# Down projections of three MLP groups as Strassen-Winograd products in a two-layer fp32 decoder step

## The reference

```python
x = x + mix
h = rms_norm(x, g_mlp[layer])
x = x + jnp.square(jax.nn.relu(h @ w_up[layer])) @ w_down[layer]
```

## Time and profile before

| | us |
|---|---|
| median of 3 runs | 1569.56 (1568.65 to 1571.38) |
| profiled execution, its own time | 1571.89 |
| profiled execution, span | 1570.2 |
| TensorE busy | 1517.2 (97%) |
| VectorE busy | 726.8 (46%) |
| ScalarE busy | 491.9 (31%) |
| GpSimd busy | 117.8 (8%) |
| granted TensorE clock, mean | 0.989 |

### The profile page before, as it was taken

How to read it: one execution, slowest core, us unless ns; L and a number is a source line. 1 busy time by engine, 2 the same in 40 slices (tenths; PEclk the granted TensorE clock), 3 DMA queues, 4 the chain that set the end, 5 groups by cost and what they waited for, 6 DMA issues and landing times.

```text
span 1570.2 us, 33444 instructions
## 1 busy us (share of the span) xinstructions
PE 1517.2 (97%) x13119; PEld 1423.2 (91%) x13119; DVE 726.8 (46%) x1265; ACT 491.9 (31%) x787; POOL 117.8 (8%) x238
## 2 busy tenths in 40 slices
PE   6999999989999999999999999898999999999996
PEld 5999867679999999999999996666999999999996
DVE  4355475635443343333543466764544434334333
ACT  5111254423332131221321116442333313213133
POOL 5310112310000000000010000222000000000000
PEclk9999999999999999999999999999999999999998
DMA  4322577732223222232242237775223222322222
GB/s 132 98 80 79 151 245 251 257 101 82 79 80 94 80 80 82 79 94 81 80 136 80 82 101 238 241 236 163 75 81 87 81 83 78 94 80 81 83 79 74
DMA packets 230949, 178.84 MB, mean 114 GB/s; under 512 B 9320, under 2 KB 202924, under 8 KB 230850
## 3 DMA queue, kind: packets, MB, share of 16 engines
q1 hardware_dynamic: 217154, 137.50, 29.9%
q0 software_dynamic: 13696, 40.00, 8.0%
HBM read 170.20 MB, written 7.26 MB: 113 GB/s over the span
## 4 chain that ended last, share of the span: by engine, by line
PE 91%; DVE 3%; SPq 2%; issue 1%; DMA 1%; ACT 1%; POOLq 0%; POOL 0%; ACTq 0%; DVEq 0%
PE B L1301 70%; PE B L1518 4%; PE B L1530 3%; PE B L1327 2%; PE B L1612 2%; PE B L1574 1%; PE B L1318 1%; PE B L1550 1%; PE B L1561 1%; SPq L382 1%; DMA WR<-in_w_in_even_dram 1%; DVE SK L1194 1%; PE B L1596 1%; PE B L1528 1%; PE B L1400 1%
## 5 line engine op out<-in xcount | busy, mean ns | idle before, releaser
L554 ACT ACTIVATE WH<-WR 128x1024 fp32r<-128x1024 f32 x175 | 184.3, 1053 | 435.1 <-PE B L1301 422.3
L822 DVE TENSOR_TENSOR WL<-WR,WH 128x1024 fp32r<-128x1024 f32 x188 | 230.2, 1224 | 57.8 <-ACT WH L544 29.0
L1301 PE MATMUL B<-ffH,WH 128*128 128x288 f32 x1024 | 219.7, 295 | 0.0
L1301 PE MATMUL B<-ffL,WH 128*128 128x288 f32 x1024 | 218.0, 294 | 0.0
L1301 PE MATMUL B<-ffH,WL 128*128 128x288 f32 x1024 | 217.5, 293 | 0.0
L1301 PE MATMUL B<-H2H,WH 128*128 128x288 f32 x960 | 205.7, 294 | 0.0
L1301 PE MATMUL B<-H2L,WH 128*128 128x288 f32 x960 | 204.2, 294 | 0.0
L1301 PE MATMUL B<-H2H,WL 128*128 128x288 f32 x960 | 203.8, 293 | 0.0
L1301 PE MATMUL B<-HH,WH 128*128 128x288 f32 x832 | 179.4, 297 | 4.1 <-DVE WL L822 2.6
L1301 PE MATMUL B<-HH,WL 128*128 128x288 f32 x832 | 178.1, 296 | 0.0
L856 DVE TENSOR_TENSOR X<-B,X 128x288 f32 (+1 forms) x160 | 65.9, 453 | 242.4 <-PE B L1301 242.1
(11 more groups left out here) (297 smaller groups left out, 1692.4 us busy)
## 6 DMA issues: line engine op xcount, KB each, us to landing
WR<-in_w_up_dram SPq DMA_DIRECT2D x64, 512.0 KB, 4.1
WR<-in_w_down_dram SPq DMA_DIRECT2D x64, 512.0 KB, 3.7
KRX<-in_cache_fox_k_dram SPq DMA_DIRECT2D x48, 256.0 KB, 4.2
WR<-in_w_in_odd_dram SPq DMA_DIRECT2D x24, 512.0 KB, 3.7
KRX<-in_cache_sb_k_dram SPq DMA_DIRECT2D x48, 256.0 KB, 3.8
VR<-in_cache_fox_v_dram POOLq DMA_DIRECT2D x44, 256.0 KB, 4.1
VR<-in_cache_sb_v_dram POOLq DMA_DIRECT2D x44, 256.0 KB, 4.7
WR<-in_w_in_even_dram SPq DMA_DIRECT2D x20, 512.0 KB, 3.9
```

The lines of the kernel that those rows point to most:

```text
L554: A(WH[1 - u][:], WR[1 - u][:], ACT.Copy).then_inc(S["w_high"], 1)
L822: V.tensor_tensor(WL[u][:], WR[u][:], WH[u][:].bitcast(F32), ALU.subtract).then_inc(S["w_low"], 1)
L1301: last = M(B[2 * u + h][:, 0:TH], w[u][:, k, :], x[:, k, h * TH:(h + 1) * TH], start=(k == 0 and n == 0), stop=(k == KT - 1 and n == 2))
```

## The change

Three of the four down groups of each layer ("seven" in the new list) are computed by Winograd's form of Strassen's scheme. For a pair of output tiles (q) the weights of a group are a 2 x 2 matrix of blocks (output tile of the pair, input tile even or odd), each 4 tiles (NQ) deep, and the hidden activations are a 2 x 2 matrix (input tile even or odd, half of the tokens). Seven products of half size replace eight: weights a11, S1 = a21 + a22, a12, S2 = S1 - a11, S4 = a12 - S2, S3 = a11 - a21, a22 against activations f11, T1 = f12 - f11, f21, T2 = f22 - T1, f22, T3 = f22 - f12, T4 = f21 - T2. Each product is 12 matmuls into one bank, and VectorE adds it to all the quarters of X that need it (`add_product`: 1152, 576, 288, 864, 288, 576 and 288 elements).

The activations' sums are made by VectorE when an up unit is evacuated (`evac_ops`, into FR, high parts OPH, low parts OPL), the weights' sums by GpSimd (into SC and ZS) from pairs of 1 MB (ZR and WRP, which lies on WR0 and WR1). ScalarE and VectorE cut each block in high and low part (`block_high`, `block_low`, 128x512 each), one pair ahead. The groups now run up and down in turn, and the seven operands fill the room that the two ff buffers had. Products are written out, not looped. The last group stays in the old form; its first unit waits for the last hidden tile only before its last chunk (`late_chunk_unit`).

```diff
+        OPH = place("OPH", [P, 7, KT // 2, TH], F32R, arena)
+        OPL = place("OPL", [P, 7, KT // 2, TH], F32R, arena + 14 * KT * TH)
+        FR = place("FR", [P, 8, TH], F32, arena + 28 * KT * TH)
+        ZH = place("ZH", [P, 7, KT // 2, P], F32R, h_addr)
+        ZL = place("ZL", [P, 7, KT // 2, P], F32R, h_addr + 14 * KT * P)
+        ZS = place("ZS", [P, 7, KT // 2, P], F32, h_addr + 14 * KT * P)
+        ZR = place("ZR", [P, KT, 2 * P], F32, h_addr + 28 * KT * P)
+        WRP = place("WRP", [P, KT, 2 * P], F32, wr_addr)
+        SC = place("SC", [P, 2, KT // 2, P], F32, tmp_addr)
...
-        MLP_ORDER = [("up", 0), ("up", 1), ("down", 0), ("up", 2), ("down", 1), ("up", 3), ("down", 2), ("down", 3)]
+        MLP_ORDER = [("up", 0), ("seven", 0), ("up", 1), ("seven", 1), ("up", 2), ("seven", 2), ("up", 3), ("down", 3)]
+        NQ = KT // 2
...
+        OP_T1, OP_11, OP_21, OP_22, OP_T2, OP_T3, OP_T4 = range(7)
...
+        PRODUCTS = [("11", OP_11), ("S1", OP_T1), ("12", OP_21), ("S2", OP_T2), ("S4", OP_22), ("S3", OP_T3), ("22", OP_T4)]
...
+        def product_bank(q, i):
+            return B[(4 + 7 * q + i) % 8]
+
...
+                    if kind == "seven":
+                        for q in range(NQ):
+                            Q = pair_no(L, grp, q)
+                            if q == 0 and grp == 0:
+                                sp.wait_ge(S["unit_done"], G_OUT[L] + KT + 1)
+                            if q == 1:
+                                sp.wait_ge(S["w_low"], g + 2)
+                            if Q >= 2:
+                                sp.wait_ge(S["block_low"], 7 * (Q - 1))
+                            sp.dma_start((ZR if q % 2 == 0 else WRP)[:, :, :], dn_v[L][grp][:, :, 2 * P * q:2 * P * (q + 1)]
+                                         ).then_inc(S[f"pair_in{q % 2}"], 16)
+                        sp.wait_ge(S["block_low"], 7 * (pair_no(L, grp, NQ - 1) + 1))
+                        continue
...
+                pool.wait_ge(S["sum_step"], (2 + 2 * L) * KT)
+                for grp in range(FG - 1):
+                    for q in range(NQ):
+                        Q = pair_no(L, grp, q)
...
+                        pool.wait_ge(S[f"pair_in{q % 2}"], 16 * (Q // 2 + 1))
+                        if Q >= 1:
+                            pool.wait_ge(S["block_low"], 7 * (Q - 1) + 2)
+                        g.tensor_tensor(s1, a21, a22, ALU.add).then_inc(S["w_sum"], 1)
+                        if Q >= 1:
+                            pool.wait_ge(S["block_low"], 7 * (Q - 1) + 4)
+                        pool.wait_ge(S["w_sum"], 4 * Q + 1)
+                        g.tensor_tensor(s2, s1, a11, ALU.subtract).then_inc(S["w_sum"], 1)
+                        if Q >= 1:
+                            pool.wait_ge(S["product"], 7 * (Q - 1) + 5)
+                        pool.wait_ge(S["w_sum"], 4 * Q + 2)
+                        g.tensor_tensor(s4, a12, s2, ALU.subtract).then_inc(S["w_sum"], 1)
+                        if Q >= 1:
+                            pool.wait_ge(S["product"], 7 * (Q - 1) + 6)
+                        g.tensor_tensor(s3, a11, a21, ALU.subtract).then_inc(S["w_sum"], 1)
...
+            def evac_ops(L, grp):
+                m0 = L * FG * KT + grp * KT
+                j0 = pair_no(L, grp, 0)
+                def body(g, i, j, u, more):
+                    next_high(g, u, more)
+                    act.wait_ge(S["relu_scaled"], i + (m0 + 1))
+                    raw = FR[:, FR_11:FR_12 + 1] if u == 0 else FR[:, FR_21:FR_22 + 1]
+                    A(raw, raw, ACT.Square).then_inc(S["relu_squared"], 1)
+                    if u == 1:
+                        act.wait_ge(S["relu_squared"], i + (m0 + 1))
+                        A(OPH[:, OP_21:OP_22 + 1, ds(j, 1), :].rearrange("p s o t -> p (s o) t"), raw, ACT.Copy).then_inc(S["op_high"], 1)
+                    act.wait_ge(S["op_sums"], j * 3 + (3 * j0 + 1 + 2 * u))
+                    lo, hi, f = (OP_T1, OP_11, FR_T1) if u == 0 else (OP_T2, OP_T4, FR_T2)
+                    A(OPH[:, lo:hi + 1, ds(j, 1), :].rearrange("p s o t -> p (s o) t"), FR[:, f:f + hi + 1 - lo], ACT.Copy).then_inc(S["op_high"], 1)
+                return body
+
+            def block_high(Q, i):
+                name = PRODUCTS[i][0]
+                if name in SUM_NO:
+                    act.wait_ge(S["w_sum"], 4 * Q + SUM_NO[name])
+                else:
+                    act.wait_ge(S[f"pair_in{Q % 2}"], 16 * (Q // 2 + 1))
+                if Q >= 1:
+                    act.wait_ge(S["product"], 7 * (Q - 1) + i + 1)
+                A(ZH[:, i], block_src(Q, i), ACT.Copy).then_inc(S["block_high"], 1)
...
+            def evac_ops(L, grp, b0=0, z=None):
+                m0 = L * FG * KT + grp * KT
+                j0 = pair_no(L, grp, 0)
+                def body(g, i, j, u, more):
+                    next_low(g, u, more)
+                    if z is not None and u == 0:
+                        norm(z)
+                    dve.wait_ge(S["unit_done"], g + 2)
+                    f0 = FR_11 if u == 0 else FR_21
+                    for h in range(2):
+                        done = V.scalar_tensor_tensor(FR[:, f0 + h], B[b0 + 2 * u + h][:, 0:TH], 0.0, R[:, h * TH:(h + 1) * TH], ALU.max, ALU.mult)
+                    done.then_inc(S["relu_scaled"], 1)
+                    dve.wait_ge(S["relu_squared"], i + (m0 + 1))
+                    if u == 0:
+                        V.tensor_tensor(FR[:, FR_T1], FR[:, FR_12], FR[:, FR_11], ALU.subtract).then_inc(S["op_sums"], 1)
+                    else:
+                        V.tensor_tensor(FR[:, FR_T2], FR[:, FR_22], FR[:, FR_T1], ALU.subtract).then_inc(S["op_sums"], 1)
+                        V.tensor_tensor(FR[:, FR_T3], FR[:, FR_22], FR[:, FR_12], ALU.subtract)
+                        dve.wait_ge(S["op_sums"], j * 3 + (3 * j0 + 2))
+                        V.tensor_tensor(FR[:, FR_T4], FR[:, FR_21], FR[:, FR_T2], ALU.subtract).then_inc(S["op_sums"], 1)
+                        low_ops(OP_21, OP_22, FR_21, j, j * 3 + (3 * j0 + 2)).then_inc(S["op_half"], 1)
+                    lo, hi, f = (OP_T1, OP_11, FR_T1) if u == 0 else (OP_T2, OP_T4, FR_T2)
+                    low_ops(lo, hi, f, j, j * 3 + (3 * j0 + (1 if u == 0 else 3))).then_inc(S["evac_dve"], 1)
+                return body
+
+            def low_ops(lo, hi, f, j, made):
+                dve.wait_ge(S["op_high"], made)
+                return V.tensor_tensor(OPL[:, lo:hi + 1, ds(j, 1), :].rearrange("p s o t -> p (s o) t"), FR[:, f:f + hi + 1 - lo],
+                                       OPH[:, lo:hi + 1, ds(j, 1), :].rearrange("p s o t -> p (s o) t").bitcast(F32), ALU.subtract)
+
+            def block_low(Q, i):
+                dve.wait_ge(S["block_high"], 7 * Q + i + 1)
+                V.tensor_tensor(ZL[:, i], block_src(Q, i), ZH[:, i].bitcast(F32), ALU.subtract).then_inc(S["block_low"], 1)
+
+            def add_product(Q, q, i):
+
+                dve.wait_ge(S["product"], 7 * Q + i + 1)
+                if i > 0:
+                    dve.wait_ge(S["product_read"], 7 * Q + i)
+                bank = product_bank(q, i)[:, 0:TH]
+                both = X[:, 2 * q:2 * q + 2, :]
...
+                V.tensor_tensor(x, bank, x, ALU.add).then_inc(S["product_read"], 1)
...
-                    if kind == "down" and grp == FG - 1:
+                    if kind == "seven":
+                        for q in range(NQ):
+                            Q = pair_no(L, grp, q)
+                            for i in range(7):
+                                add_product(Q, q, i)
+                                if q < NQ - 1:
+                                    block_low(Q + 1, i)
+                                elif i == 5:
+                                    cut_low(g, 0)
+                        continue
+                    if kind == "down":
                         for i in range(KT):
                             evac_add(2 + 2 * L)(g + i, i, i % 2, None if last and i == KT - 1 else "next")
+                    elif grp == FG - 1:
+                        unit_loop(dve, evac_up(L, grp), g, KT)
                     else:
-                        body = evac_up(L, grp) if kind == "up" else evac_add(None)
+                        body, Q = evac_ops(L, grp), pair_no(L, grp, 0)
                         if n == 0:
                             for u in range(2):
-                                evac_up(L, grp, 4, 1 + 2 * L)(g + u, u, u, "second" if u == 0 else None)
+                                evac_ops(L, grp, 4, 1 + 2 * L)(g + u, u, 0, u, "second" if u == 0 else None)
                         first = 2 if n == 0 else 0
-                        unit_loop(dve, body, g + first, KT - first, i0=first)
+                        up_loop(dve, body, g + first, first, (KT - 2 - first) // 2)
+                        block_low(Q, 0)
+                        block_low(Q, 1)
+                        body(g + KT - 2, KT - 2, NQ - 1, 0, "next")
```

(79 more changed lines are left out.)

93 lines of the change are left out of this document (67 added, 26 removed).

## The result

| | before | after |
|---|---|---|
| median, us (4 runs each) | 1570.47 | **1586.68** (1585.38 to 1588.51) |
| ratio to before, 95% interval | | 1.010 (1.0083 to 1.0117) |
| profiled execution: time / span, us | 1571.9 / 1570.2 | 1586.7 / 1584.9 |
| matmuls | 13119 | 12831 |
| VectorE busy | 46% | 60% |

The account below looks back on a forecast made before the run. TensorE's matmuls bound the kernel (busy 97%); 38.1 us saved less 22.5 us of waits is 15.6 net, 1571.9 to 1556.3, forecast 1554 us against the median. Range 1549 to 1586, 1550 to 1562 for the main case.

Parts of the forecast that it names:

- Saving, 38.1 us: Down groups on TensorE: 288 matmuls fewer at 132.2 ns each, 38.1 us.
- Rivals 3 and 4: Twelve matmuls into one bank slower, 1581, chance 0.03; products not replacing units one for one, 1575 to 1590, 0.02.
- the one on the sums: GpSimd's four weight sums per pair, 2.3 to 5.2 of 11.1 us, hidden behind the products: no cost.
- a meeting of 0.07 us: Earlier trace: a VectorE instruction sharing 0.07 us with a GpSimd select was no longer, taken against GpSimd delaying VectorE.
- Rival 1: GpSimd's sums and VectorE's two-SBUF-input instructions hold each other up: +25 us, 1579 us, chance 0.36.
- Before the last up unit: Sums delaying VectorE's four subtractions and cuts there: 2.8 us per group, six times, 17 us.
- The backlog in the products: VectorE over 11.1 us per pair when held by sums, next weights' loads late: about 1.3 x 6 = 8 us.
- last up unit: Two block cuts ahead of that unit's weight cut: 1.5 us wait, six times, 9.0 us.
- third product: Its operand is ready 3.76 us after the unit, two products cover 3.17: 0.78 with restart, six times, 4.7 us.
- products to up: Next unit's low weights cut after the sixth product's addition: 0.67 us wait, six times, 4.0 us.
- start: Start of a layer's MLP, fourth unit's weights ready at 402.8, needed at 401.8: about 1.15 us, twice, 2.3 us.
- ten units of the up loops: VectorE's longer chain for second units: about 0.25 us wait, five units in each layer, 2.5 us.

Follow-up runs that it names:

- e1: Changed kernel without GpSimd's weight sums, the blocks that need them cut from raw weight blocks: 1553.61 us, 0.9884 of the kernel before.
- e2: Changed kernel with each group's first pair loaded later and its four sums each waiting for the end of an up unit: 1555.32 us, 0.9895.
- e6: Changed kernel with timed sums, last up weights cut first, next up weights cut before the sixth addition, plus each pair's first two sums held: 1560.6 us, 0.992.
- e7: Changed kernel, timed sums, last up weights first, next up weights before sixth addition, plus first pair's fifth block cut after last up evacuation: 1553.75 us, 0.9872.
- e3: Changed kernel with the last up unit's weights cut ahead of the first pair's two blocks, sums left where they were: 1578.69 us, 1.0041.

## Why the prediction was wrong, point by point

- **Saving, 38.1 us: right.** 288 matmuls fewer, pace unchanged. Rivals 3 and 4 are out with it (132.3 ns within products, no gap at the pairs).
- **The step that failed** is the one on the sums: "Four per pair are 2.3 to 5.2 of 11.1 us, hidden too, if they only take time of GpSimd". Their length was within that (1.29 us alone, 5.2 for four; the estimate from the Trainium skill, GPSIMD Engine Reference, 3.1, was 1.2); the condition was not met, and the cost that the sum put at nothing was 33 us (e1). They also take VectorE's time wherever it has two inputs in SBUF, and the first four of each group land on the one chain without spare. The earlier trace rows had shown the meeting in one direction, and the forecast let, a meeting of 0.07 us, weigh against the other. The Trainium skill (SBUF — State Buffer, "Who interferes with whom") states the exclusion for both directions and excepts GpSimd instructions that only write; the runs agree with both (2062 beside sums, 1225 beside memsets). This rival should have been the forecast.
- **Rival 1's own sum.** Before the last up unit: 2.8 us per group expected, 3.5 measured (4.74 - 1.20, means of six), 21 us in place of 17. The backlog in the products, 8 us expected: 0. The half clock after the long wait, 12.2 us, was in no case's sum. The 8 that did not come and the 12 that nobody counted cancel in part, so this rival's 1579 comes as near as it does by luck. Without the missing term the result would lie inside the range; with it, it is 0.7 us over.
- **Waits without the sums** (e1, forecast in brackets): last up unit 1.36 us (1.5), third product 0.62 (0.78), products to up 0.64 (0.67), start 0.59 (1.15), and 0.26 with the restart in ten units of the up loops (0.25), which no list of waits shows. With the restarts 21.7 us (22.5); by the span 21.2 (1553.3 - 1532.1); and a kernel of 1553.6 (1554). The chains were counted well; only the start of an MLP was sized at twice what it costs.
- "The order of groups is thus what gives back most of the gain": true only without the sums. With them, the sums take 33 of the 53 us.

## What to carry to other kernels

Moving element-wise work to GpSimd is not free for VectorE: before placing it, list VectorE's instructions with two SBUF inputs on the critical chain, and gate GpSimd's work into the stretches where VectorE reads PSUM or is idle (e2: 31 us for a few semaphore waits). Price a long new wait of TensorE (3.4 us and more here) with the half clock behind it, not with its length alone. Look for losses in the distance of starts as well as in the list of waits, which hid 0.26 us a unit here. When a buffer's last reader sits at the end of a full engine's queue, as e6 and e7 found, delaying anything on that engine by 1 to 2 us moves the next stage's load.

## What the runs showed of the hardware

- An exclusion of VectorE and GpSimd that lasts whole instructions: 0.45 us became 1.54 beside a sum of 1.39, and sums of 1.29 became 1.74 between VectorE's cuts. A copy (one input, 0.62 us) was itself held up to 1.54 us and cost VectorE at most 0.08 in the five cuts seen; why a copy is so much milder than a sum wasn't tried.
- After each of the eleven waits of 3.4 to 4.9 us in after and e3 TensorE ran at a granted clock of 0.50 for a while, after waits of 0.4 to 1.8 us at 1.00 in the windows read. In some groups the clock fell while TensorE still stood, in others about 1 us after it had gone on (e3, first matmul at 1302.55: 1.00 until 1303.5, 0.50 from 1304.1). The cost differed from group to group (1.3 to 2.8 us for waits of 4.55 to 4.91). It was read off the windows and the spacings; no run made a long wait without the sums.
